# Turning the normalised rows of two token groups on VectorE in 32x32 blocks, with the opening and the first group put in another order

## The reference, cut to what matters

```
h  = x * (1 + sc1) + sh1                     # sc, sh, gate from silu(c) @ w_ada + b_ada
proj = h @ w_in                              # 1024 -> 2048, split into b, c, x, u, v, pool
y_a = b * conv3(c * x)                       # 256 channels
y_b = u * (W_s LN(v) + b_s)                  # 512 channels, chunks of 128 positions
y_c = pooled means over 2/4/8/16 positions, a 64x64 map per group, a scale
x  = LayerNorm(alpha * x + g1 * (concat(y_a, y_b, y_c) @ w_out))
h2 = x * (1 + sc2) + sh2
f  = square(relu(h2 @ w_up)) @ w_down        # 1024 -> 4096 -> 1024
x  = LayerNorm(alpha * x + g2 * f)
```

## Time and profile before

| | |
|---|---|
| median of 3 runs | 2038.86 us |
| profiled execution | 2037.39 us |
| its span, first to last instruction | 2035.6 us |
| mean granted TensorE clock | 0.996 of full |
| TensorE busy | 2010.5 us, 99% |
| VectorE busy | 1429.2 us, 70% |
| GpSimd busy | 1456.7 us, 72% |
| ScalarE busy | 896.0 us, 44% |
| DMA | 357.48 MB, mean 176 GB/s |

### The profile page before, as it was taken

One profiled execution on the slowest core, in us unless ns is written; L12 is line 12 of the kernel. 1 busy time (PEld: TensorE's weight loads), 2 busy tenths in 40 slices (PEclk: granted clock), 3 DMA queues, 4 the chain that ended last, 5 costly groups with the idle time before them and its releaser, 6 DMA issues.

```text
span 2035.6 us, 27636 instructions
## 1 busy us (share of the span) xinstructions
PE 2010.5 (99%) x10310; PEld 1689.6 (83%) x10310; DVE 1429.2 (70%) x1866; ACT 896.0 (44%) x1242; POOL 1456.7 (72%) x1117
## 2 busy tenths in 40 slices
PE   8999999999999999999999999999999999999996
PEld 6778888888988888888888888888888899999995
DVE  2566696785856365677888576888667778775786
ACT  3322232222133654546555544664454655444442
POOL 4446898863434677778888787888787876666686
PEclk9999999999999999999999999999999999999998
DMA  9877887943424445545345545444554534454341
GB/s 350 284 254 249 276 277 227 297 147 128 150 94 129 165 140 174 177 137 183 126 146 188 199 161 175 145 138 162 199 195 137 182 108 138 140 187 145 125 145 47
DMA packets 134623, 357.48 MB, mean 176 GB/s; under 512 B 12785, under 2 KB 46490, under 8 KB 131418
## 3 DMA queue, kind: packets, MB, share of 16 engines
q1 hardware_dynamic: 133625, 352.58, 52.5%
q10 hardware_dynamic: 864, 3.15, 0.5%
HBM read 321.22 MB, written 34.44 MB: 175 GB/s over the span
## 4 chain that ended last, share of the span: by engine, by line
PE 93%; DVE 4%; DMA 1%; ACT 1%; POOL 0%; issue 0%; SPq 0%; DVEq 0%; ACTq 0%; POOLq 0%
PE ps L1241 30%; PE ps L1243 30%; PE ps L1242 30%; DMA w_raw<-in_w_in 1%; PE ps L1490 1%; PE ps L1252 1%; PE ps L1349 1%; PE ps L1561 1%; PE ps L1269 0%; DVE acc L1842 0%; DVE hid_a L1970 0%; DVE hid_b L1970 0%; DVE pair_sums L1992 0%; DVE pair_sums L1993 0%; DVE pair_sums L1989 0%
## 5 line engine op out<-in xcount | busy, mean ns | idle before, releaser
L903 POOL TENSOR_TENSOR w_hilo<-w_raw,w_hilo 128x512 fp32r<-128x512 f32 x890 | 1279.8, 1468 | 544.9 <-ACT w_hilo L1007 544.4
L1007 ACT ACTIVATE w_hilo<-w_raw 128x1024 fp32r<-128x1024 f32 x445 | 470.3, 1058 | 521.7 <-PE ps L1243 411.5
L1241 PE MATMUL ps<-hA,w_hilo 128*128 128x512 f32 (+1 forms) x1760 | 619.9, 352 | 0.8 <-DVE acc L1876 0.8
L1242 PE MATMUL ps<-hA,w_hilo 128*128 128x512 f32 (+1 forms) x1760 | 618.3, 351 | 0.0
L1243 PE MATMUL ps<-hA,w_hilo 128*128 128x512 f32 (+1 forms) x1760 | 618.2, 351 | 0.0
L1241 PEld LDWEIGHTS ps<-hA,w_hilo 128*128 128x128 f32 x1760 | 330.3, 188 | 45.7 <-issue 2.8
L1242 PEld LDWEIGHTS ps<-hA,w_hilo 128*128 128x128 f32 x1760 | 330.3, 188 | 41.4
L1243 PEld LDWEIGHTS ps<-hA,w_hilo 128*128 128x128 f32 x1760 | 330.3, 188 | 41.3
L2078 DVE TENSOR_TENSOR acc<-acc,ps 128x512 f32<-128x512 f32 x270 | 177.7, 685 | 69.3 <-PE ps L1243 66.1
L1241 PE MATMUL ps<-w_hilo,hid_a 128*128 128x512 f32 x450 | 177.9, 395 | 0.3 <-ACT more_sums L1203 0.3
L1097 ACT ACTIVATE htmp<-ps 128x512 f32<-128x512 f32 x96 | 57.4, 598 | 272.4 <-PE ps L1243 265.2
(11 more groups left out here) (234 smaller groups left out, 2774.1 us busy)
## 6 DMA issues: line engine op xcount, KB each, us to landing
w_raw<-in_w_up SPq DMA_DIRECT2D x128, 512.0 KB, 3.5
w_raw<-w_mix SPq DMA_DIRECT2D x124, 512.0 KB, 3.2
w_raw<-in_w_down SPq DMA_DIRECT2D x97, 512.0 KB, 3.6
w_raw<-in_w_in SPq DMA_DIRECT2D x64, 512.0 KB, 4.4
xt<-in_w_ada SPq DMA_DIRECT2D x20, 1024.0 KB, 7.5
w_raw<-in_w_out SPq DMA_DIRECT2D x32, 512.0 KB, 4.5
xt<-x_norm SPq DMA_DIRECT2D x19, 512.0 KB, 5.2
xt<-in_w_down SPq DMA_DIRECT2D x36, 256.0 KB, 5.1
```

Of the source, the lines that this page charges most:

```text
L903: ins = pool.tensor_tensor(W[:, g % SLOTS, 1, cols], raw[:, g % RAW, cols], W[:, g % SLOTS, 0, cols], ALU.subtract)
L1007: act.activation(W[:, g % SLOTS, 0, :], raw[:, g % RAW, :], ACT.Copy).then_inc(hi_done, 1)
L1241: pe.matmul(out, w_hi, x_hi, start=start, stop=False)
L1242: pe.matmul(out, w_hi, x_lo, start=False, stop=False)
```

## The change: what it does

1. **Turned rows.** `TURNED = 2`: for groups 1 and 2 VectorE turns the normalised rows in 32x32 blocks (`turn_tile`, two instructions of 128x512 per tile, 16 in all) into `n_turned`, which lies in the place of `mix`. Tiles 2 and 3 are turned at the end of their own mixer behind each normalisation, tiles 0 and 1 at the start of the next mixer, ahead of its v statistics. `store_turned` writes them to a new DRAM tensor `n_blocks` (four DMAs of 512 KB behind slab 10 of the next mixer). The first write to `mix` in that mixer waits for these stores.
2. **Loads.** For groups 1 and 2 `next_n` gathers from `n_blocks` rows that are features already: eight DMAs of 32 partitions x 16 runs of 128 bytes for each buffer of `next_rows`, where one DMA of 128 rows stood. Each buffer now holds two features blocks of all 512 tokens.
3. **Features.** For groups 1 and 2 TensorE has no transposes; ScalarE's affine reads `next_rows` in SBUF directly, and waits itself for the load and for the bank. Group 3 stays as it was.
4. **Normalisation.** For groups 2 and 3 ScalarE's part of the previous group's normalisation (`o_normal`) stands one slab earlier.
5. **Opening.** Slab 1 is loaded behind piece 3 of `w_ada` in place of ahead of it; slabs 1 to 3 are rounded between the two ScalarE steps of pieces 2, 4 and 6, where they stood behind the affine of k = 1, 3, 5.
6. **First group.** The 16 later pieces of `w_ada` are spread one behind each stage of the mixer, the last ahead of slab 11 of the 12.

```
+BLK = 32
+TURNED = 2
 def ada_pieces_after(f):
-    return [ADA_FIRST + 2 * f, ADA_FIRST + 2 * f + 1] if f < 4 else [ADA_FIRST + 4 + f]
+    counts = [2, 2, 2, 1, 1, 1, 1, 2, 1, 2, 1, 0]
...
+            def store_turned(s):
+                sp.wait_ge(turned_ready, 4 * s)
+                for t in range(4):
+                    row = (s - 1) * GT + P * t
+                    sp.dma_start(n_blocks[row:row + P, :], n_turned[:, t, :]).then_inc(turned_stored, 16)
...
                 ada_weights(k)
+                if k == 3:
+                    slab(1, free=False)
                 x0_load(k)
-                if k in (2, 4):
-                    slab(k // 2, free=False)
+                if k == 4:
+                    slab(2, free=False)
...
+                    if n == 10 and s > 1:
+                        store_turned(s - 1)
...
                 elif s:
-                    sp.wait_ge(n_tr, KD * s)
+                    sp.wait_ge(n_affine, KD * s)
...
-                sp.dma_start(next_rows[t], n_rows(s + 1, t)).then_inc(n_stage, 16)
+                if s == TURNED:
+                    sp.dma_start(next_rows[t], n_rows(s + 1, t)).then_inc(n_stage, 16)
+                    return
+                sp.wait_ge(turned_stored, 64 * (s + 1))
+                blocks = n_blocks[s * GT:(s + 1) * GT, :].rearrange("(a p) f -> p a f", p=BLK)
+                for half in range(2):
+                    for c in range(P // BLK):
+                        f = 2 * P * t + P * half + BLK * c
+                        sp.dma_start(next_rows[t][BLK * c:BLK * c + BLK, GT * half:GT * half + GT].rearrange(
+                                         "p (a i) -> p a i", i=BLK),
+                                     blocks[:, :, f:f + BLK]).then_inc(n_part[t], 16)
...
             def n_features(e, k):
-                act.wait_ge(n_tr, KD * (e - SUPERS - 1) + k + 1)
-                x = ps[:, 2 + k % 2, :]
-                act.activation(x, x, ACT.Identity, bias=bias2[:, k, 0:1], scale=scale2[:, k, 0:1]
+                s, x = e - SUPERS - 1, ps[:, 2 + k % 2, :]
+                if s < TURNED:
+                    act.wait_ge(n_part[k // 2], 128 * (s + 1))
...
+                        act.wait_ge(x_split, KD * (SUPERS + s + 1) + k - 1)
+                    src = next_rows[k // 2][:, GT * (k % 2):GT * (k % 2) + GT]
+                else:
+                    act.wait_ge(n_tr, k + 1)
+                    src = x
+                act.activation(x, src, ACT.Identity, bias=bias2[:, k, 0:1], scale=scale2[:, k, 0:1]
...
                 ada_sums(k)
                 if k == 0:
                     hi_part(0, free=False)
+                if k in (2, 4, 6):
+                    hi_part(k // 2, free=False)
                 ada_turned(k)
                 x0_affine(k)
-                if k in (1, 3, 5):
-                    hi_part(k // 2 + 1, free=False)
...
-                if k is not None:
-                    n_transposes(b // BLOCKS, k)
+                if k is not None and b // BLOCKS == TURNED:
+                    n_transposes(TURNED, k)
...
+            def turn_tile(s, t):
+                step(dve.transpose(n_turned[:, t, 0:HALF], xt[:, t, 0:HALF]))
+                dve.transpose(n_turned[:, t, HALF:], xt[:, t, HALF:]).then_inc(turned_ready, 1)
...
             def mix_out(s, nt, k, x):
                 n = width(nt)
+                if s > 1 and k == MIX_ORDER[0]:
+                    dve.wait_ge(turned_stored, 64 * (s - 1))
...
+                if s > 1:
+                    for t in range(2):
+                        dve.wait_ge(xn_act, 2 * s - 1 + t)
+                        turn_tile(s - 1, t)
...
                     signal(normalise(x, x, t, ln_end), xn_dve, 2 * s + t - 1)
+                    if s in (1, 2):
+                        turn_tile(s, t)
```

More of the change, by code:

```diff
@@ L265, in ada_pieces_after @@
 def ada_pieces_after(f):
-    return [ADA_FIRST + 2 * f, ADA_FIRST + 2 * f + 1] if f < 4 else [ADA_FIRST + 4 + f]
+    counts = [2, 2, 2, 1, 1, 1, 1, 2, 1, 2, 1, 0]
+    u = ADA_FIRST + sum(counts[0:f])
+    return list(range(u, u + counts[f]))
 def mixer_stages(s, vector):
@@ L283, in mixer_stages @@
     if first:
-        out, u, held = [], ADA_FIRST, False
+        out, u = [], ADA_FIRST
         for x in a:
             out.append(x)
-            if x[0] == "F":
-                held = x[1] in (1, 2)
-                for _ in range(2 if x[1] in (0, 3) else 1):
-                    out.append(("A", u))
-                    u += 1
-                if x[1] == 0:
-                    out.append(("B", 0))
-            elif x[0] == "S" and held:
+            if x[0] == "F" and x[1] == 0:
+                out += [("A", u), ("B", 0)]
+                u += 1
+            if x != ("F", N_FM - 1):
                 out.append(("A", u))
-                u, held = u + 1, False
+                u += 1
         a = out + [("E", u - 1)]
@@ L304, in decoder_layer_kernel @@
                          y_prompt, y_sample, o_conv_p, o_pool_p, o_conv_s, o_pool_s, o_v_s,
-                         mod_rows, x_norm, w_mix):
+                         mod_rows, x_norm, n_blocks, w_mix):
     ctx = ExitStack()
@@ L489, in decoder_layer_kernel @@
         n_stage = sem("n_stage")
+        n_part = [sem(f"n_part{j}") for j in range(4)]
+        turned_ready = sem("turned_ready")
+        turned_stored = sem("turned_stored")
         n_in = [sem(f"n_in{t}") for t in range(5)]
@@ L751, in _ @@
                 u = ada_pieces_after(f)
-                if f:
+                if f and u:
                     ada_piece(u[0])
@@ L1164, in _ @@
                 for n in range(MIX_SLABS):
+                    if s and n == (2 if s > 1 else 3):
+                        o_normal(s - 1, 0)
+                        o_normal(s - 1, 1)
                     if n == 3:
-                        if s:
-                            o_normal(s - 1, 0)
-                            o_normal(s - 1, 1)
                         if nt == 5:
@@ L1178, in _ @@
                                 ada_turned(u - 1)
[L1179 to L1180 removed]
+                        if n == SLAB_O - 1:
+                            ada_turned(N_ADA - 1)
                     if n == 4 and s == 0:
```

15 lines of the change are left out of this document (8 added, 7 removed).

## The result

The changed kernel takes 2043.28 us (median of ten runs, 2041.24 to 2045.27), the kernel before on the same chip 2038.08 (median of ten too; one of them, at 10179.1 us, stands out and moves no median). The ratio is 1.0024, 95% interval 1.0016 to 1.0033: about 5 us slower, where I had forecast 2 us faster. The profiled execution took 2045.07 us, with a span of 2043.3, so its losses add up to 7.7 us against the profiled execution of before. They lie in the mixer of group 0 (2.2 us), in that of group 2 (1.5) and at the ends of groups 0 and 1 (1.6 and 1.8); no other stretch adds more than 0.3.

A forecast was written before the change was run, and what follows sets the result against it. TensorE, busy 2010.5 of 2035.6 us, was taken to bound the kernel. Gains of 0.7 + 0.6 (opening, first group) and 0.6 (group ends) took 2037.39 to 2035.5; with 1.5 for the median, 2037.0 us; range 2029.0 to 2049.0.

The forecast's parts named there:

- The turns at a group's end: Ends of groups 0 and 1: without turns, VectorE's sums bind, so 1.3 us gained per end, not 3.9.
- The price of a small load: SP's queue at the features loads: each of sixteen small DMAs takes 0.6 us to issue.
- The estimate that I made from it: From the skill's 0.95 us per 64 KB transfer: sixteen loads take 15.2 us, kernel about 2048.6 us.
- The threshold for a stall at the slabs: SP's queue behind the features slabs: sixteen loads have 11.4 us, so TensorE stalls from 0.71 us each on.
- The window: Group's end: GpSimd idle while VectorE starts its chain; if slabs come late, two instructions cost 2.1 us more.
- the middle of +1.3 and -0.8: Each group's end: between 1.3 us gained and 0.8 lost, taken as 0.3 gained, 0.6 for both.
- First group (+0.6): Group 0's mixer: spreading `w_ada` pieces removes TensorE's one wait for turned sums, 0.6 us gained.
- Opening (+0.7): Opening: rounding behind ScalarE's sums removes TensorE's waits until piece 7 of `w_ada` lands, 0.7 us gained.
- Block transposes at nothing: VectorE ahead of group 2's v statistics: eight at 0.7 us fit its 5.65 us of idle time; no cost.
- Stores at nothing: First `mix` write in group 2: turned rows land by 374.9, VectorE has 1.7 us in hand; no cost.
- late stores: Rival, group 2's mixer: stores 5 us later make TensorE wait, about +2 us, 2039 us; chance 0.07.
- slow loads: Rival, SP's queue behind slab U3: loads of 0.9 us hold up slabs, 2045.6 us, at 1.0 2052; chance 0.25.

The follow-up runs named there:

- a2: Kernel before without TensorE's turns for groups 1 and 2, plain large loads, features left unturned, no block transposes or turned stores; 2036.49 us.
- d2: Kernel before without TensorE's turns, small loads two behind each of eight slabs, VectorE's feature subtraction on 32 of 512 columns, features left unturned; 2035.74 us.
- c2: Kernel before, plain loads and TensorE's turns kept; SP holds the slab behind the last feature loads until TensorE finishes an earlier K product; 2038.47 us.
- c4: As c2, but the hold ends with VectorE's addition of the same product, about 0.9 us later; 2042.59 us.
- a1: The changed kernel with the opening and the first group as in the kernel before; 2044.42 us.
- a4: Kernel before without TensorE's turns for groups 1 and 2, with small loads, features left unturned, no block transposes or turned stores; 2041.20 us.
- b1: Kernel before with one edit: the 16 later pieces of `w_ada` spread one behind each stage of the first mixer; 2040.74 us.
- e1: The whole changed kernel, with only the sixteen small loads put two behind each of eight slabs; 2039.93 us.
- c3: As a1, with the sixteen small loads put two behind each of eight slabs; 2037.96 us.
- b2: Kernel before with the new opening alone; 2038.07 us.
- d3: As d2, with the four `pair_sums` instructions at the two group ends and the first three output sums also cut to 32 columns; 2032.55 us.
- b4: Kernel before with block transposes, turned stores and the wait of the first `mix` write, `o_normal` left where it was; 2042.65 us.

## Why the prediction was wrong, step by step

- **The turns at a group's end (+1.3 each): right in sum, by luck in its parts.** With plain loads (a2) the ends give 1.9 and 0.7 us, 2.6 in all where I had 2.6, and the run 1.3. The reason was only half right: I took VectorE's busy share as the bound, and d2 shows that less work alone gives nothing at end 0; the place of the additions in its queue counts.
- **The price of a small load (0.6 us): right,** 0.57. The Trainium skill's 0.95 ("DMA: Bandwidth & Descriptors", section Bandwidth), which I weighed, is the busy time of the DMA engines for a transfer issued from GpSimd, and not what SP was held by here; a load lands after 2.0 to 3.8 us. (The estimate that I made from it is 0.2 us too low by my own working: 3.8 us late at the slab leave 1.8 at the end, not 1.7.) The threshold for a stall at the slabs was too generous: with 0.57 each the slab behind the first pair takes 4.6 us to land where I had 3.2, and is ready at 860.0 for a product at 860.1. There was nothing left in hand, not 0.14 us per load. Still nothing was lost there.
- **The window: the step that failed.** I had worked out that issue must be over at 926.5 for GpSimd to be through with three slabs. Sixteen loads at my own 0.6 us end at 919.4 + 9.6 = 929.0, 2.5 us too late. I ought to have taken the window as lost; instead I took "the middle of +1.3 and -0.8", as if it shut by degrees. c2 and c4 show that 0.9 us decides it: set back by as much as their product starts later than in before, they issue the slab at 927.3 (window open) and 928.2 (shut), so the limit lies 0.8 to 1.7 us behind my 926.5 and still ahead of my 929.0. And I counted two of the three instructions. In the change all three grew, 3.1 us, and with that an end comes to 1.3 - 3.1 = -1.8 us; it measures 28.5 - 30.1 = -1.6 and -1.8. At the ends of group 1 in a1 and a4 only two grew, and there my -0.8 fits (-0.7 and -0.6). Where I had summed +0.6 for both ends there stand -3.4, 4.0 us of error in this one term.
- **First group (+0.6): wrong sign.** I looked at the wait that would go (0.6 us for the turned sums) and not at when each piece is issued and wanted. It costs 2.4 us in b1 and 2.3 in e1 against c3, part of which may be chance, as said there.
- **Opening (+0.7): nothing.** Piece 7's product starts at its landing, 37.41 in place of 37.82, but the first mixer starts no earlier (47.55 against 47.62). b2 is the same as before.
- **Block transposes at nothing: right in price, right by luck in effect.** 0.6 to 0.7 us each. I didn't value the earlier `o_normal` at all, and it is what makes them fit (3.5 us).
- **A wait for an input of `mix` in the mixer of group 2: not foreseen.** The mixer is 1.5 us longer in the trace of the change; c2 has the same without any edit there, so its cause stays open.
- **Stores at nothing: right** within 0.36 us. The rivals "late stores" and "slow loads" (a stall of TensorE at the slabs) didn't occur; the latter had the right place and sign, by another mechanism.

Together the terms that missed make 4.0 for the ends, 2.9 to 3.0 for the first group, 0.7 for the opening and 1.0 for the mixer part, some 8.7 us, where forecast and measurement lie 5.2 + 1.9 = 7.1 apart; the surplus is within the scatter told above.

No version beats the kernel before beyond the measurement: c3 is the best complete one, 0.6 us below it with an interval that holds 1. What the experiments leave for a further step is VectorE's queue at the group's end (d3, 5.9 us, with work left out).

## What to carry to other kernels

Where a second engine's idle time is what makes a chain fast (here GpSimd's, for VectorE), find the last moment at which its supply may come. On the late side charge the whole price on the chain's instructions, and don't take a middle: here it was 2 to 3 of three, never a half of the window. The place of DMAs in a queue can matter more than their number: the same loads cost 5 us in blocks of sixteen and nothing in pairs. And before valuing work that is taken from the critical engine, see what stands in the other engine's queue ahead of the instruction that it will wait for; its busy share doesn't tell. A wait can also cost more than its length: look at the granted clock behind it.

## What the runs showed of the hardware

- VectorE's additions and subtractions of 128x256 in float32 with both inputs in SBUF: 0.42 us with GpSimd idle, 1.3 to 1.5 beside GpSimd's subtraction of 128x512 (the first of a chain 0.5 to 1.5), and GpSimd's own is 1.27 alone. Additions of 128x512 with one input in PSUM take 0.69 us in either company.
- A load of 32 partitions by 16 runs of 128 bytes (64 KB) from DRAM holds SP for 0.49 us (median; one every 0.57) and lands 2.2 us after issue (median; 2.0 to 3.8).
- VectorE's 32x32 block transpose of 128x512 in float32: 0.67 us, one every 0.6.
- TensorE's granted clock fell from the higher to the lower level (2.4 to 1.2 GHz) for 3.4 us behind waits of 2.26 us (b4), 2.14 (a4) and 2.60 (the change, group 1), and stayed high behind waits of 2.54 and 2.62 us (the change and a1, group 0). In b4 it cost 1.4 us.
